# A gate chunk moved behind the attention heads, its last half between two groups of transposes, and one modulation half in each head slot

## The reference

```python
mod = jax.nn.silu(c) @ w_ada + b_ada                      # 6 x 1024 columns, c has one row per request group
h = x * (1 + sc1) + sh1
rq, rk, rv, rg, fq, fk, fv, ff, ga, gb = _split_in(h @ w_in + b_in)
y_ret = (jax.nn.silu(rg) * head_group_norm(o_ret, ...)) @ w_ret_proj
y_fox = fox_fn(fq, fk, fv, logf).reshape(B, L, FOX_W) @ w_fox_proj     # 16 heads of 64, softmax with forget bias
mixed = (jax.nn.sigmoid(ga) * y_ret + jax.nn.sigmoid(gb) * y_fox) @ w_o
x = layer_norm(DEEPNORM_ALPHA * x + (1 + g1) * mixed, ln1_w, ln1_b)
h = x * (1 + sc2) + sh2                                   # then 32 experts, two per token
```

## Time and profile before

| | us |
|---|---|
| median of 3 runs | 1226.48 (1223.75 to 1227.85) |
| profiled execution, its time | 1220.53 |
| its span, first to last instruction | 1218.5 |
| mean granted TensorE clock | 0.921 |
| busy: PE / DVE / ACT / POOL | 1034.2 / 901.0 / 689.4 / 187.2 |

### The profile page before, as it was taken

How to read it: one execution, slowest core, us unless ns; L and a number is a source line. 1 busy time by engine, 2 the same in 40 slices (tenths; PEclk the granted TensorE clock), 3 DMA queues, 4 the chain that set the end, 5 groups by cost and what they waited for, 6 DMA issues and landing times.

```text
span 1218.5 us, 12233 instructions
## 1 busy us (share of the span) xinstructions
PE 1034.2 (85%) x4643; PEld 771.6 (63%) x4643; DVE 901.0 (74%) x905; ACT 689.4 (57%) x699; POOL 187.2 (15%) x138
## 2 busy tenths in 40 slices
PE   5989999999999998986378878888889888888950
PEld 2668776778776755765366656666667666666730
DVE  6846434945546367578649998999999999998957
ACT  5622423332245456322358677888887888887832
POOL 0028102000000001541030331110111111110010
PEclk9899999999999989987569998999998999998975
DMA  9956644736647145834359889999999999999932
GB/s 341 292 114 147 164 79 131 190 112 150 208 153 182 57 152 180 287 115 179 141 180 361 321 313 339 364 382 397 379 389 352 379 379 382 385 380 398 347 106 101
DMA packets 86002, 304.77 MB, mean 250 GB/s; under 512 B 10180, under 2 KB 10228, under 8 KB 69046
## 3 DMA queue, kind: packets, MB, share of 16 engines
q1 hardware_dynamic: 74200, 278.56, 66.0%
q0 software_dynamic: 9440, 21.24, 5.5%
q10 hardware_dynamic: 2304, 4.20, 1.0%
HBM read 300.76 MB, written 14.73 MB: 259 GB/s over the span
## 4 chain that ended last, share of the span: by engine, by line
PE 46%; DVE 35%; issue 8%; ACT 8%; DMA 2%; SPq 0%; ACTq 0%; POOLq 0%; DVEq 0%
DVE w_lo L1635 23%; PE banks L1786 10%; PE banks L1792 9%; PE banks L1788 6%; PE banks L2118 5%; ACT w_hi L1001 4%; DVE w_lo L1122 2%; PE banks L2113 2%; PE banks L2125 2%; ACT w_hi L794 1%; PE banks L2105 1%; DVE y_pair L1662 1%; DMA w_raw<-in_w_ada 1%; PE banks L1814 1%; PE banks L1811 1%
## 5 line engine op out<-in xcount | busy, mean ns | idle before, releaser
L1635 DVE TENSOR_TENSOR w_lo<-w_raw,w_hi 128x2048 fp32r<-128x2048 f32 x189 | 436.9, 2336 | 30.9 <-ACT w_hi L1001 30.0
L1001 ACT ACTIVATE w_hi<-w_raw 128x2048 fp32r<-128x2048 f32 x189 | 356.1, 1906 | 16.0 <-PE banks L2118 16.0
L1122 DVE TENSOR_TENSOR w_lo<-w_raw,w_hi 128x2048 fp32r<-128x2048 f32 x71 | 164.5, 2329 | 63.4 <-ACT w_hi L794 63.4
L794 ACT ACTIVATE w_hi<-w_raw 128x2048 fp32r<-128x2048 f32 x71 | 134.5, 1910 | 125.7 <-PE banks L1792 116.2
L2118 PE MATMUL banks<-w_lo,xT_pair 128*128 128x512 f32 x512 | 156.8, 430 | 32.0 <-DVE w_lo L1635 30.9
L2113 PE MATMUL banks<-w_hi,xT_pair 128*128 128x512 f32 x512 | 151.6, 420 | 22.5 <-ACT w_hi L1001 20.0
L1786 PE MATMUL banks<-w_hi,h_hi 128*128 128x512 f32 x384 | 141.6, 409 | 7.9 <-DVE ret_qk L1156 5.2
L2118 PEld LDWEIGHTS banks<-w_lo,xT_pair 128*128 128x128 f32 x512 | 95.7, 200 | 82.1 <-DVE w_lo L1635 64.6
L2113 PEld LDWEIGHTS banks<-w_hi,xT_pair 128*128 128x128 f32 x512 | 98.1, 199 | 49.2 <-DVE xT_pair L1641 25.9
L731 POOL DMA_INDIRECT scratch_y<-y_pair,slot_row x16 | 36.0, 2251 | 471.3 <-DVE y_pair L1662 442.2
L1792 PE MATMUL banks<-w_lo,h_hi 128*128 128x512 f32 x384 | 106.1, 398 | 0.3 <-DVE w_lo L1122 0.3
(11 more groups left out here) (436 smaller groups left out, 1331.8 us busy)
## 6 DMA issues: line engine op xcount, KB each, us to landing
w_raw<-in_w_e_in SPq DMA_DIRECT2D x128, 1024.0 KB, 7.1
w_raw<-in_w_e_out SPq DMA_DIRECT2D x64, 1024.0 KB, 7.2
w_raw<-in_w_in SPq DMA_DIRECT2D x32, 1024.0 KB, 8.5
w_raw<-in_w_ada SPq DMA_DIRECT2D x24, 1024.0 KB, 6.6
bias_rows<-in_b_in ACTq DMA_DIRECT2D x16, 256.0 KB, 5.9
w_raw<-in_w_ret_proj SPq DMA_DIRECT2D x4, 1024.0 KB, 5.2
w_raw<-in_w_fox_proj SPq DMA_DIRECT2D x4, 1024.0 KB, 5.2
w_raw<-in_w_o SPq DMA_DIRECT2D x4, 1024.0 KB, 5.8
```

What stands on the lines that cost most here:

```text
L794: nc.scalar.activation(whi[n % NSPL][:], raw[slot_of[n]][:], ACT.Copy).then_inc(hi_done, 1)
L1001: nc.scalar.activation(whi[n % NSPL][:], raw[slot_of[n]][:], ACT.Copy).then_inc(hi_done, 1)
L1122: V.tensor_tensor(wlo[n % NSPL][:], raw[slot_of[n]][:], whi[n % NSPL][:].bitcast(F32), ALU.subtract).then_inc(lo_done, 1)
L1635: V.tensor_tensor(wlo[n % NSPL][:], raw[slot_of[n]][:], whi[n % NSPL][:].bitcast(F32), ALU.subtract).then_inc(lo_done, 1)
```

## The change

`gb1` goes behind `ada11` in `CH`. Slots 6 to 13 get one half of `ada7` to `ada10` each, slot 14 gets both halves of `ada11`, slots 15 and 16 the first half of `gb1`. The second half of `gb1` runs on PE behind the last head, between the two groups of output transposes, which both stand ahead of the first half of `pf0` now. ACT and DVE follow: the second group's splits stand ahead of the tiles of `pf1`, and `gb1` is emptied between the two groups of splits. The first group's blocks use banks 4 to 7 and so do the second's (before: 3 to 6, and 6 and 7 in turn). POOL's loads behind the heads wait for `gb1` to be emptied, in place of `ada11`. No instruction is added or removed on any engine.

```diff
-          "pr0", "pr1", "fv0", "fv1", "ada4", "gb0", "ada5", "ada6", "gb1", "ada7", "ada8", "ada9", "ada10", "ada11",
+          "pr0", "pr1", "fv0", "fv1", "ada4", "gb0", "ada5", "ada6", "ada7", "ada8", "ada9", "ada10", "ada11", "gb1",
...
-               4: [("ada5", 0, 0), ("ada5", 1, 0)], 5: [("ada6", 0, 0), ("ada6", 1, 0)], 6: [("gb1", 0, 0)],
-               7: [("gb1", 0, 1), ("gb1", 0, 2)], 8: [("gb1", 1, 0)], 9: [("gb1", 1, 1), ("gb1", 1, 2)],
-               10: [("ada7", 0, 0), ("ada7", 1, 0)], 11: [("ada8", 0, 0)], 12: [("ada8", 1, 0)], 13: [("ada9", 0, 0)],
-               14: [("ada9", 1, 0)], 15: [("ada10", 0, 0)], 16: [("ada10", 1, 0)]}
+               4: [("ada5", 0, 0), ("ada5", 1, 0)], 5: [("ada6", 0, 0), ("ada6", 1, 0)], 6: [("ada7", 0, 0)], 7: [("ada7", 1, 0)],
+               8: [("ada8", 0, 0)], 9: [("ada8", 1, 0)], 10: [("ada9", 0, 0)], 11: [("ada9", 1, 0)], 12: [("ada10", 0, 0)],
+               13: [("ada10", 1, 0)], 14: [("ada11", 0, 0), ("ada11", 1, 0)], 15: [("gb1", 0, 0)], 16: [("gb1", 0, 1), ("gb1", 0, 2)]}
...
-    for b in spare:
-        free_at[b] = (o_ok, FH)
+    for b, last in ((3, o_ok), (4, kT_cp), (5, exped), (6, exped), (7, pT_cp)):
+        free_at[b] = (last, FH)
     for k in range(4):
-        plan(("fox", k), 3 + k)
+        plan(("fox", k), 4 + k)
+    for k in range(4, KD):
+        plan(("fox", k), k)
     plan_dense("pf0")
-    for k in range(4, KD):
-        plan(("fox", k), 6 + k % 2)
...
-        pool.wait_ge(evacuated, CI["ada11"] + 1)
+        pool.wait_ge(evacuated, CI["gb1"] + 1)
...
         copy_p(FH - 1)
-        for s in range(2):
-            hi(TILE[("ada11", s)])
+        hi(TILE[("gb1", 1)])
         head_out(FH - 1)
-        hi(TILE[("pf0", 0)])
...
         split_hi("fox", foxH, range(4))
+        hi(TILE[("pf0", 0)])
+        split_hi("fox", foxH, range(4, KD))
         hi(TILE[("pf1", 0)])
-        split_hi("fox", foxH, range(4, KD))
...
-        for s in range(2):
-            lo(TILE[("ada11", s)])
-            if s == 0:
-                drain("ada10")
+        lo(TILE[("gb1", 1)])
         normalised(8, FH)
-        drain("ada11")
-        lo(TILE[("pf0", 0)])
...
         split_lo("fox", 1, foxH, foxL, range(4))
+        lo(TILE[("pf0", 0)])
+        evac_z("gb1")
+        split_lo("fox", 1, foxH, foxL, range(4, KD))
         lo(TILE[("pf1", 0)])
-        split_lo("fox", 1, foxH, foxL, range(4, KD))
...
         weighted(FH - 1)
-        ada(11)
...
         blocks_T("fox", fox_rows, range(4))
+        half("gb1", 1, actH, actL)
         pe.wait_ge(fox_norm, 2)
+        blocks_T("fox", fox_rows, range(4, KD))
         half("pf0", 0, foxH, foxL, split_ready("fox"))
-        blocks_T("fox", fox_rows, range(4, KD))
         half("pf1", 0, foxH, foxL)
```

More of the change, by code:

```diff
@@ L933, in _ @@
                 hi(n)
-            if h == 5:
+            if h == 13:
                 bias_rows("gb1")
```

## The result

The changed kernel takes 1207.8 us (median of 4 runs) beside 1225.1 for the kernel before; ratio 0.985, 95% interval 0.983 to 0.987. The forecast was 1212.4 with a range from 1208 to 1220: the sign was right, and the time lies just under the range. The profiled execution of after took 1206.94 us, span 1205.0. Between the two profiled executions the difference is 13.6 us, near the 14.06 of the sum; between the medians it is 17.4. The fit of the profiles is less of a success than it looks, and the gap to the medians needs an explanation.

A forecast was written before the change was run, and what follows sets the result against it. PE was taken to bound the heads, through its own work, waits and matmuls at lower clock behind them. Removed terms 1.31 + 2.19 + 5.50 + 0.54 + 4.52 = 14.06 us, from the median 1226.48, gave 1212.4 us, range 1208 to 1220.

The forecast's parts named there:

- Slot 10: Head slot 10: PE's wait until DVE has emptied gb1, whose bank ada7 needs, goes; 1.31 us.
- slot 16 and ada11: Slot 16 and ada11: PE's waits of 1.08 and 1.11 us for a w_lo both go; 2.19 us.
- the splits: Behind the last head: 3.04 us of PE waiting for splits and 2.46 of half clock go; 5.50 us.
- the bank: Second group of output transposes: PE's wait for a bank used twice goes; 0.54 us.
- Light slots: Slots 6 to 13, one modulation half each: cost between 0 and 1.8 us, 0 taken.
- Rivals 2 and 4: 2: new waits in light slots, 1219.0 us, chance 0.10; 4: PE's clock falls there, 1232.3 us, chance 0.04.
- Slot 12: PE's wait of 1.23 us behind the first division stays, as does the slow slot behind it, 9.03 against 6.63 us.
- Rival 5: The wait in slot 12 and its slow slot go as well, 1.23 + 2.40; 1208.8 us, chance 0.08.
- The merge: PE's merge transposes behind pf0: waits shrink and half clock goes, emptying of pf0 covered by 1.7 us; 4.52 us.
- Rival 1: The merge wait stays, POOL's arithmetic lying over the emptying of pf0; 1216.9 us, chance 0.18.
- rival 3: DVE held off by POOL in four operations of the emptying of pf0, 12.4 us more; 1226.5 us, chance 0.04.
- POOL: POOL's loads and arithmetic behind the last head: residual has 12 us of cover, so waiting for gb1 costs nothing.

The follow-up runs named there:

- heads_alone: Against after: new head-slot table kept, second half of gb1 right behind the last weighted sum, transposes, splits and banks behind the heads as in before; 1212.8 us.

## Why the prediction was right and wrong, step by step

*Slot 10, slot 16 and ada11, the splits, the bank: 1.31 + 2.19 + 5.50 + 0.54.* All these waits are gone from after, and heads_alone brings the last two back (2.11 of the 3.04 us, and 0.55). Right. Only slot 10 was too small: in four of six profiles of before the half clock adds 11.43 - 9.87 = 1.56 us, which the first profile, the one read, did not have.

*Light slots: 0.* Right: slots 6 to 11 take 6.63 to 6.65 us each, no gap, clock 1.00. Slots 13 and 14, put at 0 too, show no wait. Rivals 2 and 4 did not come.

*Slot 12.* The wait stayed, as said, but "as does the slow slot behind it" was wrong: 6.69 us in place of 9.03. The step took one profile's clock for a property of the code. Before shows the slow slot in three profiles of six, after in none of four. From head 0 to the end of the last head 9.5 us went (143.4 to 133.94), not 6.1, and this is most of the difference. Rival 5 priced the slot, but tied it to the wait. Why after never falls there is not settled: wait and surroundings look alike.

*The merge: 4.52 us.* This is the term that failed, and the forecast's own sign of being wrong, a merge wait named after gate, is there. From the merge wait to wo0 only (1.21 + 8.09) - (1.75 + 7.27) = 0.28 us went; against the average of the six profiles of before it is 1.6, and 0.7 of waiting for w_lo ahead. DVE began the emptying at 496.30, 30.2 us behind the last head, where 29.8 was forecast, and PE wanted it at 40.3, where 40.1 was. But the 8.6 us for emptying pf0 were carried over from before, and with POOL's operations at another phase it took 11.8: 1.7 us of cover less 3.2. Rival 1 is what happened, by the mechanism of rival 3, whose price was too high: three operations and not four, about 2.0 us each. The cause named in the step, DVE's late start behind two w_lo, was in good part POOL's even in before: without POOL's work the same two w_lo stood ahead but took 4.49 us in place of 6.71, DVE began 29.6 us behind the last head in place of 31.5 and was through in 6.9 us in place of 8.6, and PE had no wait for gate.

*POOL.* Its loads took 488.79 - 478.18 = 10.6 us and not 16.9, so its arithmetic began 22.7 us behind the last head and not at 28.4, and ended at 46.4 and not at 55.6. The residual never waited for it, as forecast.

*The base.* The sum was made on one profile and taken from a median 5.95 us above it. That carries over only if an execution 6 us slower loses them elsewhere. It did not: part lay in the removed waits. Over six profiles before takes 234.28 us on average in the stretch, 1.8 above the first; after takes 219.3. So the change is worth 15.0 us there, and some more in the places that it touches, since slot 4, outside it, was 0.5 us slower on average in the profiles of after. The other 2.4 us of the medians' 17.4 are not found: outside the stretch the profiles of the two show no difference (head 0 starts at 332.1 to 335.5 us in before and at 332.2 to 337.0 in after), and timed runs of before spread from 1217 to 1231 us. The profiled executions say the same as the stretch: 1223.8 us on average in six of before, 1208.9 in four of after, 14.9 apart. What the runs without a profile have beyond that stays open.

*The steps that failed, in short.* The emptying of pf0 was put at 8.6 us and took 11.8, so the merge gave 0.28 us and not 4.52. The slow slot behind slot 12 was put at 0 and gave 2.34 us. The base, one profile for a kernel whose profiles differ by 3.75 us, was the third. The time lies 4.6 us below the forecast: 1.4 by the base's median (1226.48 of three runs, 1225.1 with a fourth), 0.9 by the stretch (15.0 in place of 14.06), and 2.4 open.

## What to carry to other kernels

Before a wait is priced, take several profiles: a kernel that waits for a race between two engines has not one cost but a spread. Here the spread was 3.75 us in six profiles of before and 0.12 in four of after, though after keeps some of the waits. When work is moved, do not carry over an operation's duration from the old place; look which engine runs beside it in the new one, and whether the traces show that the two hold each other up: here DVE with two SBUF inputs did beside POOL's TENSOR_TENSOR, and hardly beside its TENSOR_SCALAR. And where an engine off the path slows one on it, moving its work helps only if the new place has neither such operations nor a deadline: three of the four places tried here gave back more than half of the gain.

## What was not expected of the hardware

The granted clock behind one and the same wait fell in some executions and not in others: behind the 1.31 us in slot 10 the four matmuls took 1.14 us in two profiles of before and 1.42 to 1.58 in four, with the same instructions ahead. Two operations that lock each other out cost the loser what is left of its partner's time, in both directions: 0.69 against 2.7 us on DVE, 2.4 against 4.9 on POOL, 4.5 against 8.3 for two conversions of a weight tile. And which POOL operation it is matters: a TENSOR_TENSOR held DVE up in 56 cases of 56, a TENSOR_SCALAR, which reads SBUF as well, by more than 0.13 us in one of 17.
